# The first AdaLN shift as TensorE products, row by row with the first norm, in a float32 transformer kernel

## The chip, the cores and the metric

One core of a Trainium2 chip runs the whole program in one launch. The metric is the device time in microseconds of one execution, the median of several. The core has five engines with queues of their own: TensorE (PE; matmuls, with a weight load PEld for each), VectorE (DVE), ScalarE (ACT), GpSimd (POOL) and SyncE (SP, which here issues all the transfers from HBM). They meet only at semaphores.

## The reference

Three transformer blocks on x of 256 positions by 1024 features, in float32. The two first blocks are modulated by a vector c. What matters here:

```python
cond = jax.nn.silu(c)                                   # (1, 1024)
for l in range(2):
    m = (cond @ w_mod[l] + b_mod[l]).reshape(bsz, 3, 3, D_MODEL)
    x = x + 0.5 * m[:, 0, 2][:, None] * swiglu(adaln_in(x, norm_g[l, 0], m, 0), w1, w3, w2)
    ...

def adaln_in(x, g, m, i):
    return rmsnorm(x, g) * (1 + m[:, i, 1][:, None]) + m[:, i, 0][:, None]

def swiglu(h, w1, w3, w2):
    return (silu(h @ w1) * (h @ w3)) @ w2
```

Each layer needs 9 x 1024 modulation values: for each of its three sublayers a shift (index 0), a scale (1) and a gate (2), each value a dot product of 1024 terms with the silu of c. The first feed-forward layer (FFN 0) can't begin before its 1024 shifts and 1024 scales are known.

## The kernel before, in words

Features lie on the 128 partitions in 8 chunks, positions along the free axis: X is 128 x (8 x 256). A float32 product is made of three fp32r products: ScalarE rounds a block of weights into its high part WH (the split, L1287), VectorE makes the low part WL (L1860), activations have XH and XL likewise, and TensorE adds XH WH, XL WH and XH WL. WH and WL hold four units of 128 x 1024 each.

All weights come as one stream of items of up to 128 x 3072 (1.5 MB), in the order in which they are used, and SyncE issues them one after another; a wait in front of one holds up all behind it. FFN item c holds w1 and w3 of hidden chunk c and w2 of chunk c-1, and goes to one of three slots of `ring` (L611). FFN item 0 has only w1 and w3, 1 MB. Between them come modulation items (L600): three rows each, a row being the 128 x 1024 block whose 128 sums give one column of `modv`. They go to the slots scr (two of them), PR, att and kf_mix, which later hold other data, and item 5 borrows the third slot of `ring`. Items 0 to 5 make up the head: the first 8 rows of the stream are the shifts of sublayer 0, the next 8 the scales, then 2 rows of gates.

On VectorE `mod_row` (L1910 to 1923) handles a row by one multiply-and-reduce with the silu of c (`cond`, broadcast to all partitions), line L1916. For the head it does 16 of them one after another, then `scale_rates` (L1925) makes the gains adav, `norm_scale` (L1891) scales the 8 chunks of X by gain and reciprocal root into SQ, ScalarE adds the shift and rounds to XH (L1338, the high), VectorE makes XL (L1907, the low). The root itself is ScalarE's: squares (L1311), summed over features by TensorE with a matrix of ones (L674), then logarithm and exponential (L1325, L1328).

TensorE in the head: the sum of the squares, 8 `keep_warm` matmuls on constants (L668) in three groups behind waits, and then `head_up` (L719): 16 products XH WH chunk by chunk (L726), 16 XH WL (L731), 16 XL WH (L736). From chunk 1 of the FFN on, `up` (L691, L692, L695) and `down` (L785, L787, L792) alternate. ScalarE rounds FFN item c+1 before the silu of chunk c, and VectorE takes three more modulation rows for each chunk between its lows, gate rows of the head first. The wait in front of FFN item 2 (L609) is for the last scale row:

```python
i = PLACE[name]
if i == RING - 1:
    sp.wait_ge(*at("scale_row_read"))
```

Of the kernel before, what the change touches and what calls it, by code (L numbers as in the profile page):

```python
# [26 lines left out]
HEAD_MODS = 6  # L27
PADL, PADR = 3, 3
# [11 lines left out]
def columns(spec):  # L40
# [8 lines left out]
    ("b_mod", 144), ("norm_g", 48), ("a_qg", 1), ("a_kg", 1), ("c_qg", 1), ("c_kg", 1),  # L49
# [144 lines left out]
def build(nc, stream, param_d, const_d, bias_d, filter_d, x_d, mem_d, pos_d, c_d, out_d, known):  # L194
# [83 lines left out]
    def landed(name):  # L278
# [3 lines left out]
        if name[0] == "mod":  # L282
            k = MOD_SLOT[name[1]]
            return sig.sem(f"mod_landed{k}"), 16 * sum(MOD_SLOT[i] == k for i in range(name[1] + 1))
# [39 lines left out]
    def low_of(u):  # L324
        return f"low_{low_engine(u)}", u

# [252 lines left out]
    with nc.Block() as block:  # L579
# [3 lines left out]
        def _(sp):  # L583
            sp.dma_start(cond[:, :], c_d.partition_broadcast(P)).then_inc(*mark("c_in", n=16))
            sp.dma_start(par[:, :], param_d).then_inc(*mark("par_in", n=16))
            for name, n in ITEMS:
                if name[0] == "mod":
# [11 lines left out]
                    n = D if i == HEAD_MODS - 1 else n  # L599
# [15 lines left out]
                if name == ("ffn", 0, 0):  # L615
                    i = HEAD_MODS - 1
                    sp.wait_ge(*at("mod_read", 0))
                    sp.dma_start(mod_slots[0][:, D:ITEM], stream[ITEM_AT["mod", i], :, D:ITEM]).then_inc(*mark("gate_rows_in", n=16))
                if name == ("mod", 1):
                    sp.dma_start(con[:, 0:2 * P], const_d[:, 0:2 * P]).then_inc(*mark("ones_in", n=16))  # L620
                if name == ("mod", 3):
                    sp.dma_start(X, x_d).then_inc(*mark("x_in", n=16))
                if name == ("ffn", 0, 2):
                    sp.wait_ge(*at("mod_read", 4))
# [24 lines left out]
        def _(pe):  # L649
# [27 lines left out]
            def ffn(f):  # L677
# [41 lines left out]
                def head_up(b, units):  # L719

                    for k in range(KD):
                        pe.wait_ge(*at("norm_high", key, k))
                        for a, u in units:
                            if k == 0:
                                pe.wait_ge(*at("high", u))
                            pe.matmul(b[:, a * S:(a + 1) * S], part(WH, u, k), XH[:, k, :], start=(a == 0 and k == 0), stop=False,  # L726
                                      skip_group_check=True)
                    for a, u in units:
                        pe.wait_ge(*at(*low_of(u)))
# [1999 lines left out]
```

## Time and profile before

| what | value |
|---|---|
| median of 3 runs | 1420.14 us (1418.20 to 1420.48) |
| the profiled execution | 1419.84 us |
| its span, first to last instruction | 1418.0 us |
| TensorE busy | 1353.5 us, 95% |
| VectorE, ScalarE, GpSimd busy | 1089.7, 692.5, 53.8 us |
| moved by DMA | 305.79 MB, mean 216 GB/s |
| granted TensorE clock, mean | 0.992 of full |

Times of the trace are counted from the start of the span; the execution lasts 1.84 us longer than its span. Busy times overlap between engines, so they don't add up to the span. An engine that shows idle time is late only if the next thing on the chain of waits is its own.

### The profile page before, as it was taken

How to read it: one execution, taken by the hardware profiler on the slowest of the kernel's cores; microseconds unless marked ns; L12 is line 12 of the kernel's file. 1: busy time of each engine (PE TensorE's matmuls, PEld its weight loads, DVE VectorE, ACT ScalarE, POOL GpSimd, SP SyncE). 2: the span in 40 equal slices, each digit the busy share in tenths (PEclk: the TensorE clock that was granted, in tenths of full speed). 3: DMA queues.
4: the chain of work that ended last, by engine and by line, in shares of the span. 5: the costliest groups of instructions: out<-in, count | busy, mean ns of one | idle time of the engine just before them, and what ended most of it. 6: DMA issues, size and time to landing. Idle time of an engine off the chain costs nothing.

```text
span 1418.0 us, 26072 instructions
## 1 busy us (share of the span) xinstructions
PE 1353.5 (95%) x10734; PEld 1290.7 (91%) x10734; DVE 1089.7 (77%) x1835; ACT 692.5 (49%) x1120; POOL 53.8 (4%) x57
## 2 busy tenths in 40 slices
PE   2999999999999999999999999999999989999998
PEld 2999999889999999999998799999997868899998
DVE  6888999987787889878778866565678767677776
ACT  3443435555443363334465553344487756544453
POOL 0000000001000000001000020000010030100000
PEclk9999999999999999999999999999999999999999
DMA  9997758256768576574753145655422324245551
GB/s 392 409 388 288 309 187 337 104 192 277 304 267 317 217 289 267 223 326 172 283 200 134 60 179 216 240 194 212 176 93 105 119 78 175 90 178 182 186 196 62
DMA packets 32182, 305.79 MB, mean 216 GB/s; under 512 B 3480, under 2 KB 5784, under 8 KB 7360
## 3 DMA queue, kind: packets, MB, share of 16 engines
q1 hardware_dynamic: 32064, 304.13, 55.7%
q8 instruction: 85, 1.39, 0.4%
q14 instruction: 33, 0.27, 0.1%
HBM read 303.05 MB, written 1.06 MB: 214 GB/s over the span
## 4 chain that ended last, share of the span: by engine, by line
PE 83%; DVE 8%; DMA 3%; ACT 3%; issue 2%; POOL 1%; SPq 0%; POOLq 0%; DVEq 0%; ACTq 0%
PE bank L695 14%; PE bank L691 13%; PE bank L692 13%; PE bank L868 13%; PE bank L787 7%; PE bank L785 7%; PE bank L792 6%; DVE WL L1860 2%; DMA kf_mix<-in_stream 2%; PE bank L674 2%; DMA ring<-in_stream 1%; PE bank L709 1%; PE bank L941 1%; PE bank L715 1%; PE bank L952 1%
## 5 line engine op out<-in xcount | busy, mean ns | idle before, releaser
L1860 DVE TENSOR_TENSOR WL<-ring,WH 128x1024 fp32r<-128x1024 f32 x414 | 496.7, 1223 | 58.4 <-ACT WH L1287 56.2
L1287 ACT ACTIVATE WH<-ring 128x1024 fp32r<-128x1024 f32 x414 | 424.5, 1054 | 137.1 <-PE bank L868 51.9
L691 PE MATMUL bank<-XH,WH 128*128 128x256 f32 x1648 | 401.6, 282 | 0.6 <-ACT WH L1287 0.6
L692 PE MATMUL bank<-XL,WH 128*128 128x256 f32 x1648 | 400.0, 281 | 0.0
L691 PEld LDWEIGHTS bank<-XH,WH 128*128 128x128 f32 x1648 | 310.1, 188 | 6.5 <-issue 6.0
L692 PEld LDWEIGHTS bank<-XL,WH 128*128 128x128 f32 x1648 | 310.1, 188 | 0.5 <-issue 0.5
L695 PE MATMUL bank<-XH,WL 128*128 128x256 f32 x1648 | 229.9, 282 | 2.1 <-DVE WL L1860 2.1
L695 PEld LDWEIGHTS bank<-XH,WL 128*128 128x128 f32 x1648 | 210.2, 189 | 2.3 <-DVE WL L1860 2.3
L785 PE MATMUL bank<-GH,WH 128*128 128x256 f32 x840 | 203.6, 280 | 0.0
L787 PE MATMUL bank<-GL,WH 128*128 128x256 f32 x840 | 203.4, 280 | 0.0
L1372 ACT ACTIVATE SG<-bank 128x256 f32<-128x256 f32 x84 | 32.3, 384 | 340.7 <-PE bank L695 336.3
L787 PEld LDWEIGHTS bank<-GL,WH 128*128 128x128 f32 x840 | 158.5, 189 | 0.0
L785 PEld LDWEIGHTS bank<-GH,WH 128*128 128x128 f32 x840 | 158.4, 189 | 0.0
L1987 DVE TENSOR_TENSOR tmp<-SG,bank 128x256 f32<-128x256 f32 x88 | 37.0, 421 | 135.8 <-ACT SG L1372 134.8
L792 PE MATMUL bank<-GH,WL 128*128 128x256 f32 x808 | 111.4, 279 | 0.0
L792 PEld LDWEIGHTS bank<-GH,WL 128*128 128x128 f32 x808 | 102.2, 188 | 0.0
L868 PE MATMUL bank<-XH,WH 128*128 128x256 f32 x512 | 84.4, 290 | 4.2 <-ACT XH L1336 1.4
L868 PEld LDWEIGHTS bank<-XH,WH 128*128 128x128 f32 x512 | 70.6, 188 | 11.8 <-issue 7.8
L868 PE MATMUL bank<-XH,WL 128*128 128x256 f32 x512 | 80.1, 282 | 0.0
L1973 DVE SCALAR_TENSOR_TENSOR scr<-bank,par,scr 128x255 f32<-128x255 f32 x88 | 38.5, 478 | 46.8 <-ACT scr L1362 46.1
L1809 POOL TENSOR_TENSOR SQ<-SQ 128x256 f32<-128x256 f32 x35 | 36.9, 1055 | 935.1 <-ACT SQ L1311 934.0
L868 PE MATMUL bank<-XL,WH 128*128 128x256 f32 x512 | 71.5, 282 | 0.0
(321 smaller groups left out, 1598.5 us busy)
## 6 DMA issues: line engine op xcount, KB each, us to landing
ring<-in_stream SPq DMA_DIRECT2D x128, 1536.0 KB, 6.6
scr<-in_stream SPq DMA_DIRECT2D x15, 1536.0 KB, 9.9
PR<-in_stream SPq DMA_DIRECT2D x15, 1536.0 KB, 9.6
att<-in_stream SPq DMA_DIRECT2D x15, 1536.0 KB, 9.8
ring<-in_stream SPq DMA_DIRECT2D x12, 1024.0 KB, 4.9
ring<-in_stream SPq DMA_DIRECT2D x10, 512.0 KB, 3.6
kf_mix<-in_stream SPq DMA_DIRECT2D x2, 1536.0 KB, 16.9
con<-in_consts SPq DMA_DIRECT2D x1, 1680.0 KB, 20.0
```

The costliest lines, as they stand in the source:

```text
L691: pe.matmul(o, part(WH, u, k), XH[:, k, :], start=(k == 0), stop=False)
L692: pe.matmul(o, part(WH, u, k), XL[:, k, :], start=False, stop=False)
L695: last = pe.matmul(o, part(WL, u, k), XH[:, k, :], start=False, stop=(k == KD - 1))
L785: pe.matmul(out(m), part(WH, u, m), GH[:, c % 2, :], start=(c == 0 and m % 2 == 0), stop=False, skip_group_check=True)
L787: pe.matmul(out(m), part(WH, u, m), GL[:, c % 2, :], start=False, stop=False, skip_group_check=True)
L792: last = pe.matmul(out(m), part(WL, u, m), GH[:, c % 2, :], start=False, stop=False, skip_group_check=True)
L868: last = pe.matmul(bank[b][:, 0:S], part(w, u, blk + k), x[:, k, :], start=(opens and k == (ks or [0])[0]), stop=(p == parts[-1] and k == ...
L1287: act.activation(part_all(WH, u), raw(u), ACT.Copy).then_inc(*mark("high", u))
L1809: ins = pool.tensor_tensor(SQ[:, 0, :], SQ[:, 0, :], SQ[:, c, :], ALU.add)
L1860: dve.tensor_tensor(part_all(WL, u), raw(u), part_all(WH, u).bitcast(F32), ALU.subtract)\
L1973: ins = dve.scalar_tensor_tensor(o, src, prm("fconv_w", 2 * NFF * k + col), o, ALU.mult, ALU.add)
L1987: dve.tensor_tensor(G32[h], SG[h, c % 2, :], second, ALU.mult).then_inc(*mark("g32", f, c))
```

## The change

The 1024 shifts of sublayer 0 are no longer reduced on VectorE. Their weights lie in the stream as 8 blocks of 8 x (128 x 128), with the contracted features on partitions. POOL fills `wide`, the last 1024 columns of kf_mix, with the silu of c, each feature's value repeated over 128 columns (eight operations). TensorE multiplies: eight matmuls of 128 columns in plain float32 for each block of 128 shifts, which gives the block's shifts in each of the 128 columns; ScalarE adds b_mod to one column of them. The scales stay reductions on VectorE.

The stream's head alternates scale row and shift row. Each row is a transfer of its own (512 KB) into one of 16 places, in flight up to six at a time: row j waits until row j-6 is used. x, the ones and FFN item 0 are issued ahead of them. The first norm goes chunk by chunk on all engines as the rows come, with the products of FFN chunk 0 in between; the keep-warm matmuls of the head are removed.

The waits in SyncE's queue ahead of the items behind the head are for the single rows that used their places, and for the last row on the same semaphore.

SyncE, from the start of the program, before (slots scr, PR, att, kf_mix and ring; `mod_read` is a modulation item reduced, `low_dve` a low made):

```order
L584 DMA cond<-in_c 128x1024
L585 DMA par<-in_params 128x570
L600 DMA scr<-in_stream 128x3072 x2
L620 DMA con<-in_consts 128x256
L600 DMA PR<-in_stream 128x3072
L600 DMA att<-in_stream 128x3072
L622 DMA X<-in_x 128x2048
L600 DMA kf_mix<-in_stream 128x3072
L600 DMA ring<-in_stream 128x1024
L611 DMA ring<-in_stream 128x2048
L618 DMA scr<-in_stream 128x2048 [waits mod_read]
L600 DMA PR<-in_stream 128x3072 [waits mod_read]
```

and now, from the rows on (rows 0 to 15, of which six are left out, the gate rows, modulation item 6, FFN item 1, modulation item 7, FFN item 2):

```order
L610 DMA scr<-in_stream 128x1024 x6
L610 DMA PR<-in_stream 128x1024 [waits scale_in]
L610 DMA PR<-in_stream 128x1024 [waits shift_sum]
...
L610 DMA ring<-in_stream 128x1024 [waits shift_sum]
L613 DMA scr<-in_stream 128x2048 [waits shift_sum,scale_in]
L634 DMA PR<-in_stream 128x3072 [waits scale_in,shift_sum]
L645 DMA ring<-in_stream 128x3072
L634 DMA att<-in_stream 128x3072 [waits shift_sum,scale_in]
L645 DMA ring<-in_stream 128x3072 [waits shift_sum]
```

Six rows start freely, ten wait each for a row six places earlier, and modulation item 6 (PR, L634), with FFN item 1 behind it, waits for rows as well: for the reduction of row 14 (`scale_in`) among them.

TensorE's head, now (kf_mix is `wide`, scr and PR hold shift rows):

```order
L701 MATMUL bank<-SQ,con 128x256 [waits squared] x7
L754 MATMUL bank<-kf_mix,scr 128x128 [waits c_wide,mod_landed1]
L754 MATMUL bank<-kf_mix,scr 128x128 x7
L754 MATMUL bank<-kf_mix,scr 128x128 [waits mod_landed3]
L754 MATMUL bank<-kf_mix,scr 128x128 x7
L764 MATMUL bank<-XH,WH 128x256 [waits high,norm_high]
...
L754 MATMUL bank<-kf_mix,scr 128x128 [waits mod_landed5,shift_in]
L754 MATMUL bank<-kf_mix,scr 128x128 x7
L764 MATMUL bank<-XH,WH 128x256 [waits norm_high]
L764 MATMUL bank<-XH,WL 128x256
```

The products of a chunk (and the low products of the one before) now stand between two shift products, which share one in-order queue with them; 64 shift matmuls came in and 8 keep-warm ones went.

The diff, cut to its core, in the order of the file (SyncE, TensorE, ScalarE, POOL, VectorE):

```diff
+    def front_row(n):
+        a = (n % MOD_ROWS) * D
+        return mod_slots[n // MOD_ROWS][:, a:a + D]
+    wide = kf_mix[:, 3 * D:4 * D]
...
+            sp.dma_start(con[:, 0:2 * P], const_d[:, 0:2 * P]).then_inc(*mark("ones_in", n=16))
+            sp.dma_start(X, x_d).then_inc(*mark("x_in", n=16))
+            first = ("ffn", 0, 0)
+            sp.dma_start(slot(first), stream[ITEM_AT[first], :, 0:COLS[first]]).then_inc(sig.sem("slot_landed0"), 16)
+            for j in range(2 * KD):
+                if j >= FRONT:
+                    sp.wait_ge(*at("shift_sum" if j % 2 else "scale_in", (j - FRONT) // 2))
+                a = (j % MOD_ROWS) * D
+                sp.dma_start(front_row(j), stream[ITEM_AT["mod", j // MOD_ROWS], :, a:a + D]).then_inc(*mark(f"mod_landed{j % FRONT}", j, n=16))
...
-                        sp.wait_ge(*at("mod_read", HEAD_MODS - 1 if p == 0 else p))
+                        for w in front_read(p) if p < HEAD_MODS else [("mod_read", p)]:
+                            sp.wait_ge(*at(*w))
+                        if p < HEAD_MODS:
+                            j = max(j for j in range(2 * KD) if j % FRONT == k)
+                            sp.wait_ge(*at("shift_sum" if j % 2 else "scale_in", j // 2))
...
                     if i == RING - 1:
-                        sp.wait_ge(*at("scale_row_read"))
+                        sp.wait_ge(*at("shift_sum", KD - 1))
...
+                    def shift(k):
+                        take(k % 2, "shift_in", k)
+                        pe.wait_ge(*at(f"mod_landed{(2 * k + 1) % FRONT}", 2 * k + 1))
+                        if k == 0:
+                            pe.wait_ge(*at("c_wide"))
+                        for d in range(KD):
+                            last = pe.matmul(bank[k % 2][:, 0:P], front_row(2 * k + 1)[:, d * P:(d + 1) * P], wide[:, d * P:(d + 1) * P],
+                                             start=(d == 0), stop=(d == KD - 1))
+                        last.then_inc(*mark("shift_sum", k))
...
+                    for k in range(KD):
+                        shift(k)
+                        if k > 0:
+                            products(k - 1)
+                        if k > 1:
+                            low_products(k - 2)
+                    products(KD - 1)
+                    low_products(KD - 2)
+                    low_products(KD - 1)
...
             norm(("sub", 0, 0))
-            keep_warm(3)
-            pe.wait_ge(*at("stat_root", ("sub", 0, 0)))
-            keep_warm(3)
-            pe.wait_ge(*at("ada_in", 0, 0))
-            keep_warm(2)
...
+                for k in range(KD):
+                    act.wait_ge(*at("scale_in", k))
+                    g = prm("norm_g", k)
+                    act.activation(adav[:, 0, 0, k:k + 1], modv[:, KD + k:KD + k + 1], ACT.Identity, scale=g, bias=g)\
+                        .then_inc(*mark("rate_in", k))
+                    act.wait_ge(*at("shift_sum", k))
+                    act.activation(modv[:, k:k + 1], bank[k % 2][:, 0:1], ACT.Identity, bias=prm("b_mod", k))\
+                        .then_inc(*mark("shift_in", k))
+                    if k > 0:
...
+                        highs(k0, [k - 1])
...
+            for d in range(KD):
+                ins = pool.tensor_scalar(wide[:, d * P:(d + 1) * P], ones, prm("c_cols", d), None, ALU.mult)
...
+            def front_norm():
+                k0, (u0, u1) = ("sub", 0, 0), up_units(0, 0)
+                scale_row(0)
+                split_to(u0)
+                scale_row(1)
+                split_to(u1)
+                norm_root(k0)
+                for k in range(1, KD + 1):
+                    if 1 < k < KD:
+                        scale_row(k)
+                    dve.wait_ge(*at("rate_in", k - 1))
+                    norm_scale(k0, [k - 1])
+                    if k > 1:
+                        norm_lows(k0, [k - 2])
+                norm_lows(k0, [KD - 1])
```

## Rows read from the trace of the kernel before

**Rows 1.** The page, busy us by engine (share of the span, instructions).

```profile
PE 1353.5 (95%) x10734; PEld 1290.7 (91%) x10734; DVE 1089.7 (77%) x1835; ACT 692.5 (49%) x1120; POOL 53.8 (4%) x57
```

**Rows 2.** Stages: length, busy PE, PEld, DVE, ACT, POOL, clock, DMA share, GB/s.

```profile
10.00:20.00 10.00, 0.00 (x0) 0.00 (x0) 9.77 (x17) 0.00 (x0) 0.00 (x0) 1.00 1.01 426
...
28.00:31.00 3.00, 2.66 (x16) 2.26 (x16) 3.00 (x7) 0.89 (x2) 0.00 (x0) 1.00 0.99 421
...
40.00:50.00 10.00, 9.63 (x80) 9.33 (x79) 5.85 (x10) 4.64 (x6) 0.00 (x0) 1.00 1.02 378
```

**Rows 3.** Timeline of SyncE's queue: start us, us, queue, line, issue.

```profile
21.62 0.43 SPq L611 DMA_DIRECT2D ring<-in_stream  x1
...
32.23 0.33 SPq L611 DMA_DIRECT2D ring<-in_stream  x1
```

**Rows 4.** Timeline of ScalarE, 23 to 51 us; in brackets idle before, and releaser.

```profile
23.64 2.56 ACT L1311 ACTIVATE SQ<-X 128x256 f32<-128x256 f32 x8 [16.15 <-DMA X<-in_x]
...
29.81 0.47 ACT L1325 ACTIVATE tmp<-bank,par 128x256 f32<-128x256 f32 x1 [2.31 <-PE bank L674]
...
31.02 2.00 ACT L1287 ACTIVATE WH<-ring 128x1024 fp32r<-128x1024 f32 x2 [0.29 <-DMA ring<-in_stream]
...
41.03 2.01 ACT L1287 ACTIVATE WH<-ring 128x1024 fp32r<-128x1024 f32 x2 [4.68 <-DMA ring<-in_stream]
...
49.99 1.06 ACT L1287 ACTIVATE WH<-ring 128x1024 fp32r<-128x1024 f32 x1 [4.30 <-DMA ring<-in_stream]
```

**Rows 5.** Chain that ended last, 0 to 75 us: start us, us, what.

```profile
5.07 22.20 DMA kf_mix<-in_stream
...
29.79 1.20 DVE kf_mix L1916
...
32.23 17.74 DMA ring<-in_stream
```

**Rows 6.** Timeline of TensorE, 29 to 60 us.

```profile
29.61 0.83 PE L668 MATMUL bank<-con 128*128 128x128 f32 x6
...
39.54 2.23 PE L736 MATMUL bank<-XL,WH 128*128 128x256 f32 x16
...
49.83 1.10 PE L792 MATMUL bank<-GH,WL 128*128 128x256 f32 x8
...
51.19 0.36 PE L691 MATMUL bank<-XH,WH 128*128 128x256 f32 x1 [0.26 <-ACT WH L1287]
...
58.23 1.69 PE L695 MATMUL bank<-XH,WL 128*128 128x256 f32 x8 [2.06 <-DVE WL L1860]
```

**Rows 7.** Timeline of VectorE: first reduction, scaled chunks, lows of the third FFN chunk.

```profile
9.96 1.28 DVE L1916 CUSTOM_DVE_ANT_0 scr<-scr,cond,par 128x1024 f32<-128x1024 f32 x1 [9.96 <-DMA scr<-in_stream]
...
32.52 3.26 DVE L1895 SCALAR_TENSOR_TENSOR SQ<-X,adav,tmp 128x256 f32<-128x256 f32 x8
...
65.11 2.35 DVE L1860 TENSOR_TENSOR WL<-ring,WH 128x1024 fp32r<-128x1024 f32 x2
```

**Rows 8.** Single lines: count, ns min/median/max, first and last start.

```profile
L1392 ACT ACTIVATE rates<-rates x1: 212/212/212, 168.0 to 168.0; 128x8 f32<-128x8 f32 x1
...
L1809 POOL TENSOR_TENSOR SQ<-SQ x35: 721/746/1473, 226.0 to 1220.0; 128x256 f32<-128x256 f32 x35
```

**Rows 9.** The page, DMA issues: count, KB each, median us to landing.

```profile
ring<-in_stream SPq DMA_DIRECT2D x128, 1536.0 KB, 6.6
...
ring<-in_stream SPq DMA_DIRECT2D x10, 512.0 KB, 3.6
```

**Rows 10.** Stages again, for the granted clock (third number from the end).

```profile
35.00:38.00 3.00, 3.00 (x15) 3.00 (x16) 3.00 (x5) 1.35 (x4) 0.00 (x0) 0.50 1.00 421
...
60.00:62.00 2.00, 2.00 (x11) 2.00 (x11) 2.00 (x4) 2.00 (x3) 0.00 (x0) 0.50 1.04 442
...
230.00:235.00 5.00, 3.95 (x33) 3.79 (x33) 4.34 (x11) 4.42 (x11) 0.00 (x0) 1.00 1.00 391
1095.00:1100.00 5.00, 3.72 (x10) 2.91 (x11) 3.64 (x7) 4.94 (x6) 0.00 (x0) 0.64 0.38 160
```

More of the change, by code:

```diff
@@ L27 @@
 HEAD_MODS = 6
+FRONT = 6
 PADL, PADR = 3, 3
@@ L283, in landed @@
             k = MOD_SLOT[name[1]]
-            return sig.sem(f"mod_landed{k}"), 16 * sum(MOD_SLOT[i] == k for i in range(name[1] + 1))
+            front = sum(j % FRONT == k for j in range(2 * KD))
+            return sig.sem(f"mod_landed{k}"), 16 * (front + sum(MOD_SLOT[i] == k for i in range(HEAD_MODS, name[1] + 1)))
         i = PLACE[name]
@@ L719, in head_up, with products, low_products @@
                 def head_up(b, units):
-                    for k in range(KD):
+                    def shift(k):
[7 more added lines that the diff above has]
+                        last.then_inc(*mark("shift_sum", k))
+                    def products(k):
                         pe.wait_ge(*at("norm_high", key, k))
                         for a, u in units:
[L724 to L729, printed above, removed]
-                        for k in range(KD):
-                            pe.matmul(b[:, a * S:(a + 1) * S], part(WL, u, k), XH[:, k, :], start=False, stop=False,
-                                      skip_group_check=True)
-                    for k in range(KD):
+                            for which, w in ((WH, ("high", u)), (WL, low_of(u))):
+                                if k == 0:
+                                    pe.wait_ge(*at(*w))
+                                pe.matmul(b[:, a * S:(a + 1) * S], part(which, u, k), XH[:, k, :],
+                                          start=(which is WH and a == 0 and k == 0), stop=False, skip_group_check=True)
+                    def low_products(k):
                         pe.wait_ge(*at(*normed(key, k)))
@@ L1328, in root, with highs @@
                 act.activation(norm_rstd(k), norm_rstd(k), ACT.Exp, scale=-0.5).then_inc(*mark("stat_root", k))
-            def highs(k):
+            def highs(k, which=None):
                 N = NORMS[k]
-                for c in range(N["n"]):
+                for c in which or range(N["n"]):
                     act.wait_ge(*at("scaled", k, c))
@@ L1619, in _ @@
             act.activation(cond[:, :], cond[:, :], ACT.Silu).then_inc(*mark("cond"))
+            act.activation(prm("c_cols", 0, 8), prm("c_cols", 0, 8), ACT.Silu).then_inc(*mark("c_cols"))
+            def front_norm():
+                k0, (u0, u1) = ("sub", 0, 0), up_units(0, 0)
+                load_rates()
+                squares(k0, lambda c: [("x_in",)])
+                split_to(u0)
+                root(k0)
+                split_to(u1)
[8 more added lines that the diff above has]
+                    if k > 0:
+                        if k == 1:
+                            act.wait_ge(*at("shift_in", 0))
+                        act.wait_ge(*at("shift_in", k - 1))
+                        highs(k0, [k - 1])
+                act.wait_ge(*at("shift_in", KD - 1))
+                highs(k0, [KD - 1])
+                split_to(u1)
             for l in range(2):
                 if l == 0:
-                    norm(("sub", 0, 0), lambda c: [("x_in",)], ahead=up_units(0, 0)[1])
+                    front_norm()
                 else:
@@ L1896, in norm_scale, with norm_lows @@
                                              ALU.mult, ALU.mult).then_inc(*mark(*scaled(k, c)))
-            def norm_lows(k):
+            def norm_lows(k, which=None):
                 N = NORMS[k]
-                for c in range(N["n"]):
+                for c in which or range(N["n"]):
                     dve.wait_ge(*at("norm_high", k, c))
@@ L2622, in lay_out @@
     put_p("b_mod", feature_cols(f["b_mod"]))
+    put_p("c_cols", feature_cols(f["c"]))
     put_p("norm_g", feature_cols(f["norm_g"]))
@@ L2659, in lay_out @@
             blocks["mod", MOD_ITEMS * l + k] = m[k]
+    m = f["w_mod"][0]
+    rows = []
+    for k in range(KD):
+        rows.append(m[:, D + k * P:D + (k + 1) * P].T)
+        rows.append(m[:, k * P:(k + 1) * P].reshape(KD, P, P).transpose(1, 0, 2).reshape(P, D))
+    rows += [m[:, 2 * D + k * P:2 * D + (k + 1) * P].T for k in range(2)]
+    for k in range(HEAD_MODS):
+        blocks["mod", k] = np.stack(rows[MOD_ROWS * k:MOD_ROWS * (k + 1)], 1)
     def ffn(n, w1, w3, w2):
```

48 lines of the change are left out of this document (27 added, 21 removed).

## The prediction

> **What bounds the kernel now.** The page comes first: the span is 1418.0 us and TensorE is busy 95% of it [rows 1], so over the whole run only less TensorE work, or less TensorE waiting, shortens it. The edit removes hardly any work, so the question is what TensorE waits for near the start. The stage table answers: from 10 us on, and still at 40 to 50, the DMA engines are busy all the time, at 426 and 378 GB/s [rows 2]. That is a full pipe: what lands by when is set by the bytes ahead of it. The queue of SyncE shows FFN items 1 and 2 issued at 21.62 and 32.23 us [rows 3], and ScalarE waits for items 0, 1 and 2 to land: 31.02, 41.03 and 49.99 us [rows 4]. The chain of waits agrees: the kf_mix item, reductions behind it, then a DMA from 32.23 that takes 17.74 [rows 5]; its last waits lie at 51 and 58 us, and from there on TensorE has no gap worth naming. So the span is "landing of FFN item 2, plus a fixed rest", and FFN item 1 has no slack ahead of it either: the head's last products start at 39.54 and take 2.23 (to 41.77), item 1's first product needs the split that starts at 41.03 and takes 1.06 [rows 4, 6].
>
> **What the change can't give.** Ahead of FFN item 1 stand the same bytes before and after: c, parameters, ones, x, FFN item 0, sixteen rows of 512 KB, gate rows, modulation item 6. The eight VectorE reductions that go (1.20 us apart [rows 5]) were done while the pipe filled. Finishing the head sooner than 41.77 therefore gives nothing: item 1 can't land before 41.03. What the change can do is leave the pipe empty, because rows 6 to 15, and above all the PR item (modulation item 6) with FFN item 1 behind it, are now issued only after waits on single rows.
>
> **When the waits open.** Arrival is no limit: row 15 has the same bytes ahead of it as FFN item 0 had, so it would land at 31.0 and row 14 at 29.8 (512 KB at 426 GB/s is 1.23 us). x now has 2.0 MB up to its end against 2.4 MB for the first scr item, which landed at 9.96 [rows 7], so x lands at about 9.0. Squares to summed norm took 29.81-23.64 = 6.17 us [rows 4], so the sum is ready at 15.15. TensorE then does shift products 0 and 1. Each is 8 f32 matmuls of 128 columns, two records each; six such records took 0.83 [rows 6], hence 0.11 apart with a tail of 0.17. So 32 records take 3.5 us, and shift sum 1 is there at 18.8. (Row 3 is there at about 16.4; ScalarE's split of w3 ends at 17.2, VectorE's low of it at 18.4, its first scaled chunk at 18.8.)
> From there a loop closes: shift product k, ScalarE's bias copy of one column, ScalarE's high of chunk k-1, then TensorE's four products of chunk k-1 and two low ones, which stand ahead of shift product k+1. One turn is 16x0.11+0.17 = 1.93, the copy 0.25 (0.21 from SBUF [rows 8], taken a little higher from PSUM), the high 0.44 and six products 0.71 (eight take 1.10, of which the last 0.28 [rows 6]: 0.118 each), and hand-overs 0.15: **3.5 us per row pair** against 2.46 us of DMA. Shift sum 2 comes at 22.0, 4 at 29.0, 5 at 32.5. VectorE needs 1.20+0.41+0.41 = 2.0 per turn (0.41 for a scaled chunk [rows 7], and as much for a low) but waits for the same highs: row 14's reduction follows the low of chunk 4, so it ends at 32.5+0.25+0.44+0.45+1.28 = 34.9.
> That frees the PR item: its wait names the reduction of row 14. The pipe is dry by then: row 15 is issued at shift sum 4 (29.0), the gate rows behind it, 1.5 MB, done by about 34. The PR item and FFN item 1 go out together at 35.0. From an empty pipe 512 and 1536 KB take 3.6 and 6.6 us to land [rows 9], which is 2.4 and 2.9 us plus the bytes; 3 MB need 2.4+7.4 = 9.8, so item 1 lands at 44.8 instead of 41.03: **+3.7 us**. FFN item 2 is free at shift sum 7 (39.5), while the pipe is still full, and is late by the same 3.7; so is the rest.
>
> **What TensorE's clock gives back.** TensorE finishes the head at about 41.3 and idles until 45.8. After its 2 us idle at 56 to 58 the granted clock was 0.50 from about 58.6 to 62.2, the lower level of 1.2 GHz, and likewise around 35 to 38 after a stretch of short pieces [rows 10]; either costs half of 3.4 us, 1.7. I take it that item 1's products run at the lower level for as long. That is covered: two waits stand behind them, 0.26 us at 51.19 and 2.06 us at 58.23, where VectorE's low of w3 is last [rows 6]. With 1.7 of these 2.3 us used up, only 0.6 us of idling is left at that place, and gaps of 0.3 to 0.6 at 41.8 and 51 brought no fall of the clock. So the fall at 58.6 goes: **-1.7 us**. VectorE keeps up: the low of the next w3 (65.11 and the 1.2 of the first of the pair [rows 7], plus 3.7: 70.0) is ready when TensorE wants it, at about 70.2.
>
> **The small parts.** The eight broadcasts of POOL start when the ones and the silu of c are there (7.7) and must end by 15.15. At 0.75 us, the median of POOL's two-input operations of twice the columns [rows 8], they end at 13.7: hidden. At the 1.47 us of the slowest of these they end at 19.5 and cost up to 4 us: kept for the range. Nothing here excludes either. ScalarE's 16 one-column activations are in the loop above; the extra silu and the eight removed keep-warm matmuls lie beside waits. Rows of 4 KB a partition instead of 12 KB: nothing, since while the 512 KB row and the 1 MB item drained before 31 us the pipe moved 421 GB/s [rows 2]. The Trainium skill ("DMA: Bandwidth & Descriptors", on the latency of a transfer) gives each DMA about 2 us of fixed cost beside its bytes; paid one after another by sixteen rows, the sum by that page would hold an estimated 32 us more. In this trace such costs overlap while several transfers are queued: the DMA share is full [rows 2].
>
> **The sum.** 1419.84 + 3.7 - 1.7 = 1421.8. The profiled execution is 0.3 below the median of 1420.14; I put the median to come at **1422.0**. A measurement of this kernel can tell about 0.2%, 2.8 us, from no change: no change lies between 1417.3 and 1423.0. The DMA term's ends: 0 if the loop keeps up with arrival (reduction of row 14 at 31.05, plus 9.8, is 40.9), and +16 if each turn ran at the lower clock (1.93 and 0.71 doubled: 5.9 us a turn; shift sum 5 near 46).
>
> **The rivals.**
> 1. *The pipe stays full* (0.11). If a turn takes 2.5 us, item 1 lands at 41.0 to 42.5, and with the second fall of the clock gone or not the time is 1418.5 to 1420.5. For it: VectorE's 2.0 us a turn. Against: the products alone are 2.6 us of a turn.
> 2. *The clock falls in the head: slower* (0.22). TensorE works some 2.7 of 3.5 us. It held the full clock at 3.95 of 5 us busy, and lost it at 3.72 of 5 [rows 10]. It decides as soon as one fall lies between 19 and 32 us: each adds up to 1.7 us to the loop and so to the landing, two or three give 1424 to 1428. The late POOL broadcast ends in the same place. The Trainium skill ("TensorE: Matmul & The Clock Gate", Part 1) says that the lower clock is the default and that only activity lifts it. By that rule the head's pauses speak for this rival. Rows 10 show a case of either kind.
> 3. *The fall at 58 us stays* (0.15): item 1's products start at full clock, or the wait at 58 keeps its 2 us. Then nothing is given back: 1423.5.
> 4. *Faster by over 0.2%* (0.06): landings come out earlier than bytes allow at 426 GB/s, or both falls go and VectorE's chain after 50 us shortens too: 1416.
> The forecast case (item 1 late by 2.5 to 4.9 us, the fall gone: 1420.6 to 1423.2) has 0.46.
>
> **How the numbers follow.** Range: 1418.8 to 1427.0. It leaves out about half of rival 4 and of rival 1's lower end, and the tail of rival 2. Within 0.2%: nearly all of the forecast case and rival 1, 0.55. Slower: rivals 2 and 3 and a rest, 0.38. Faster: 0.07.
>
> **What would show it.** In the profile after: x lands near 9 and the norm's sum ends near 15; shift products come 3.5 us apart; SyncE issues PR at about 35 with a dip of the DMA share just then; ScalarE's wait for FFN item 1 ends near 44.8 and for item 2 near 53.7; a lower clock at 45 to 49 and none at 62. I am wrong if the DMA share has no dip between 22 and 37 us, if turns are nearer 2.5 or 5 us, or if w1 of item 2 is not later than 49.99.

## Result, and the profile after

| what | before | after |
|---|---|---|
| median of 4 runs each, one chip | 1420.06 us | **1427.35 us** (1426.14 to 1429.87) |
| ratio | | 1.0057 [1.0045, 1.0069] |
| the profiled execution, its span | 1419.84, 1418.0 us | 1428.07, 1426.1 us |
| TensorE busy | 1353.5 us | 1369.9 us |
| granted clock, mean | 0.992 | 0.992 |

The change makes the kernel slower by 7.3 us. The forecast was 1422.0, with a range up to 1427.0. A slower kernel had been given a chance of 0.38; the size lies outside the range.

The page of the changed kernel, span and busy times (they answer to [rows 1]):

```profile
span 1426.1 us, 26338 instructions
PE 1369.9 (96%) x10846; PEld 1307.5 (92%) x10846; DVE 1079.8 (76%) x1818; ACT 696.6 (49%) x1137; POOL 58.4 (4%) x65
```

The head first. Timeline of SyncE's queue in the changed kernel (start us, us, queue, line, issue), to set beside [rows 3]:

```profile
29.54 0.33 SPq L610 DMA_DIRECT2D ring<-in_stream  x1
29.98 0.36 SPq L613 DMA_DIRECT2D scr<-in_stream  x1
35.52 0.33 SPq L634 DMA_DIRECT2D PR<-in_stream  x1
35.90 0.43 SPq L645 DMA_DIRECT2D ring<-in_stream  x1
```

Row 15 and the gate rows go out at 29.5 and 30.0, then nothing until 35.52, where the PR item and FFN item 1 follow. Timeline of ScalarE after, against [rows 4]:

```profile
15.69 0.47 ACT L1364 ACTIVATE tmp<-bank,par 128x256 f32<-128x256 f32 x1 [2.79 <-PE bank L701]
...
26.05 0.26 ACT L1674 ACTIVATE modv<-bank,par 128x1 f32<-128x1 f32 x1 [2.59 <-PE bank L754]
...
29.55 0.26 ACT L1674 ACTIVATE modv<-bank,par 128x1 f32<-128x1 f32 x1 [2.57 <-PE bank L754]
...
45.62 2.00 ACT L1326 ACTIVATE WH<-ring 128x1024 fp32r<-128x1024 f32 x2 [4.49 <-DMA ring<-in_stream]
...
54.59 1.06 ACT L1326 ACTIVATE WH<-ring 128x1024 fp32r<-128x1024 f32 x1 [4.32 <-DMA ring<-in_stream]
...
72.67 0.38 ACT L1411 ACTIVATE SG<-bank 128x256 f32<-128x256 f32 x1 [0.22 <-PE bank L722]
```

The copies that add the bias to two neighbouring shifts (26.05, 29.55) lie 3.50 us apart: one turn of the loop. FFN items 1 and 2 land at 45.62 and 54.59, 4.6 us later than before (41.03, 49.99). The stages after (columns as in [rows 2]):

```profile
14.00:20.00 6.00, 5.25 (x41) 4.88 (x39) 5.24 (x8) 3.19 (x8) 0.00 (x0) 1.00 1.03 411
20.00:26.00 6.00, 5.25 (x42) 4.88 (x42) 4.90 (x11) 1.32 (x4) 0.00 (x0) 1.00 1.02 392
...
34.00:36.00 2.00, 2.00 (x19) 2.00 (x19) 1.83 (x4) 0.00 (x0) 0.00 (x0) 1.00 0.51 213
36.00:38.00 2.00, 1.25 (x11) 1.06 (x11) 0.74 (x2) 0.93 (x3) 0.00 (x0) 1.00 0.78 188
...
46.00:48.00 2.00, 1.27 (x6) 1.27 (x7) 1.29 (x2) 1.98 (x3) 0.00 (x0) 0.50 1.05 449
...
60.00:62.00 2.00, 2.00 (x20) 2.00 (x19) 1.93 (x6) 0.29 (x1) 0.00 (x0) 1.00 0.95 390
```

The pipe of transfers runs dry at 34 to 38 us (213 and 188 GB/s). TensorE's granted clock is 0.50 at 46 to 48 and full at 60 to 62, where [rows 10] had 0.50.

So far this is the forecast. Its price shows where the silu of each FFN chunk starts, since that follows the chunk's last product. The silu of chunk 0 is 4.59 us later than before, that of chunk 3 only 3.13 (72.67 against 69.54). But from there the difference grows without a new wait in the head: 4.1 us at 215 us, 4.8 at 529, 5.8 at 1016, 8.05 at the last chunk, near 1409. Of these 4.9 us, 4.5 come in FFN 0, 1, 3 and 4, 0.06 us with each chunk. The rest isn't even: between 1118 and 1234 us, ahead of FFN 4, another 1.4 come, where the granted clock was at 0.50 for 10.2 us instead of 6.8, and the remaining stretches take 1.0 back. Two rows of ScalarE's timeline before, two neighbouring chunks:

```profile
103.62 0.39 ACT L1372 ACTIVATE SG<-bank 128x256 f32<-128x256 f32 x1 [4.58 <-PE bank L695]
112.14 0.38 ACT L1372 ACTIVATE SG<-bank 128x256 f32<-128x256 f32 x1 [4.57 <-PE bank L695]
```

and the same chunks after:

```profile
106.98 0.39 ACT L1411 ACTIVATE SG<-bank 128x256 f32<-128x256 f32 x1 [4.57 <-PE bank L722]
115.56 0.39 ACT L1411 ACTIVATE SG<-bank 128x256 f32<-128x256 f32 x1 [4.57 <-PE bank L722]
```

A chunk took 8.52 us and takes 8.58, with the same instructions. TensorE's timeline shows which of them grew. The first row is the first of the 16 `down` products with WH, the second the 8 with WL behind them. Before:

```profile
121.60 0.28 PE L785 MATMUL bank<-GH,WH 128*128 128x256 f32 x1
...
123.48 1.10 PE L792 MATMUL bank<-GH,WL 128*128 128x256 f32 x8
```

After:

```profile
125.09 0.28 PE L829 MATMUL bank<-GH,WH 128*128 128x256 f32 x1
...
127.01 1.12 PE L836 MATMUL bank<-GH,WL 128*128 128x256 f32 x8
```

The sixteen take 1.88 us before and 1.92 after, at a granted clock of 1.00 in both. By the mean distance from one product's start to the next one's, between 100 and 220 us: the products of `up` have 118.3 to 118.9 ns in both kernels, those of `down` 117.9, 117.8 and 117.8 before (GH WH, GL WH, GH WL), and 121.3, 118.8 and 120.2 after. With the 840, 840 and 808 of them that is an estimated 2.8 + 0.8 + 1.9 = 5.6 us (with the unrounded means). It is more than the 4.5 us that the chunks show, since in FFN 2 (529 to 716 us) the difference hardly grows.

No wait of the head reaches so far. What can is in a line that my prediction passed over, and that the cut diff doesn't show: the vector c that POOL reads as `c_cols` is 8 new columns of the parameter tile `par` (570 to 578 columns).

```diff
-    ("b_mod", 144), ("norm_g", 48), ("a_qg", 1), ("a_kg", 1), ("c_qg", 1), ("c_kg", 1),
+    ("b_mod", 144), ("c_cols", 8), ("norm_g", 48), ("a_qg", 1), ("a_kg", 1), ("c_qg", 1), ("c_kg", 1),
```

The tiles are laid out one behind another, so every tile behind `par` begins 32 bytes further on: XH and XL, GH and GL among them, but not WH and WL.

### The profile page after: what moved, and what is told of

The parts are those of the page before. It is cut to its first block, busy times and chain, and to the rows that moved or that the text cites. A ratio compares the mean times of both kernels' runs of the same rounds, so it can differ in the third digit from the quotient of the medians.

```text
span 1426.1 us, 26338 instructions
## 1 busy us (share of the span) xinstructions
PE 1369.9 (96%) x10846; PEld 1307.5 (92%) x10846; DVE 1079.8 (76%) x1818; ACT 696.6 (49%) x1137; POOL 58.4 (4%) x65
## 4 chain that ended last, share of the span: by engine, by line
PE 87%; DVE 6%; ACT 3%; issue 2%; DMA 1%; POOL 1%; POOLq 0%; DVEq 0%; SPq 0%; ACTq 0%
PE bank L912 14%; PE bank L722 13%; PE bank L718 13%; PE bank L719 13%; PE bank L829 7%; PE bank L831 7%; PE bank L836 7%; PE bank L701 2%; DVE WL L1930 1%; PE bank L736 1%; PE bank L754 1%; DMA ring<-in_stream 1%; PE bank L985 1%; PE bank L742 1%; PE bank L996 1%
## 5 line engine op out<-in xcount | busy, mean ns | idle before, releaser
L719 PE MATMUL bank<-XL,WH 128*128 128x256 f32 x1648 | 401.2, 282 | 0.0
L722 PEld LDWEIGHTS bank<-XH,WL 128*128 128x128 f32 x1648 | 210.6, 189 | 0.7 <-DVE WL L1930 0.7
L831 PE MATMUL bank<-GL,WH 128*128 128x256 f32 x840 | 206.3, 282 | 0.0
L912 PEld LDWEIGHTS bank<-XH,WL 128*128 128x128 f32 x512 | 71.2, 191 | 0.3 <-issue 0.2
```

The source lines that it names most:

```text
L719: pe.matmul(o, part(WH, u, k), XL[:, k, :], start=False, stop=False)
L722: last = pe.matmul(o, part(WL, u, k), XH[:, k, :], start=False, stop=(k == KD - 1))
L831: pe.matmul(out(m), part(WH, u, m), GL[:, c % 2, :], start=False, stop=False, skip_group_check=True)
L912: last = pe.matmul(bank[b][:, 0:S], part(w, u, blk + k), x[:, k, :], start=(opens and k == (ks or [0])[0]), stop=(p == parts[-1] and k == ...
```

## The experiments

Three theories at the start. **A**: the head costs some 3 us, and the rest is where the operand tiles lie. **B**: the rest comes with the longer program, wherever the tiles lie. **C**: it is something else that the new head leaves behind. Beside them, that the growth is chance of one profile. Each ratio below is to the kernel before on the same chip, with its 95% interval.

### The tiles moved, the head left alone

```diff
-    ("eps", 1), ("inv", 1), ("halfpi", 1), ("tiny", 1)])
+    ("eps", 1), ("inv", 1), ("halfpi", 1), ("tiny", 1), ("spare", 8)])
```

> The kernel before with 8 unused columns at the end of its parameter tile, and nothing else: every tile that is allocated behind it lies 32 bytes later, as in the changed kernel. In the changed kernel an FFN chunk of 72 products takes 8.58 us instead of 8.52, over some 84 chunks, about 5 us. Theory A (the place of the operands in memory): this kernel takes 1425 us, 5.0 more than before, and its chunks take 8.58. Theory B (the longer TensorE program) and theory C (something that the new head leaves behind): it takes 1420.1, chunks at 8.52.

Measured: 1423.63 us (11 runs), ratio 1.0026 [1.0018, 1.0035]. Chunks take 8.58 us, `down` products 121.4 and 120.2 ns; the difference to before is 0.5 us at chunk 3 and 5.4 at the last. Eight unused columns, and no change of the head, give the growth from chunk to chunk. By the runs they cost 3.7 us [2.6, 5.0]; the profiled execution is the slowest of the 11.

### The changed kernel with its tiles back in place

In the changed kernel, ("spare", 56) at the same place: 64 new columns in all, so every tile has the place it had before, give or take a whole 256 bytes.

> The changed kernel with 56 unused columns at the end of its parameter tile, so that all tiles behind it lie 256 bytes later than in the kernel before instead of 32. Theory A: chunks at 8.52 again, 1422.3 us, 5.0 less than the changed kernel; what is left against before, about +2 to +3, is the head. Theories B and C: no change, 1427.3.

Measured: 1423.92 us (9 runs), ratio 1.0028 [1.0018, 1.0038]. Chunks take 8.52 us; the difference is 2.7 us at chunk 3 and 3.0 at the last. The groups of TensorE in the changed kernel (line, products | busy us, mean ns of one):

```profile
L829 PE MATMUL bank<-GH,WH 128*128 128x256 f32 x840 | 206.2, 284 | 0.0
...
L836 PE MATMUL bank<-GH,WL 128*128 128x256 f32 x808 | 113.5, 282 | 0.0
```

and of this kernel:

```profile
L829 PE MATMUL bank<-GH,WH 128*128 128x256 f32 x840 | 202.5, 279 | 0.0
...
L836 PE MATMUL bank<-GH,WL 128*128 128x256 f32 x808 | 111.4, 279 | 0.0
```

So C is out: the new head with the tiles back in place has no growth. The parts add up within their intervals: the head alone 0.28%, the place alone 0.26%, together 0.54% beside 0.57 measured. By the runs the head costs 4.0 us [2.6, 5.4], by this one profile 3.0.

### A longer program without the tiles moved

```diff
             pe.wait_ge(*at("ones_in"))
+            keep_warm(56)
             norm(("sub", 0, 0))
```

> The kernel before with 56 more matmuls on constants ahead of the sum of the squares, while TensorE has nothing to do: as many as the changed head has more. Theory B (TensorE's program is longer, so later instructions lie elsewhere in it): chunks of 8.58 us and 1425 us. Theories A and C: 1420.1, since the 56 matmuls end before x lands.

Measured: 1418.84 us (11 runs), ratio 0.9998 [0.9990, 1.0007]; chunks take 8.52 us. TensorE has the 10846 instructions of the changed kernel here, so B is out, and chance was out with the first experiment. In this profile the clock is 1.00 at 35 to 38 and at 60 to 62 us, where [rows 10] had 0.50; the silu of chunk 0 came 1.2 us later all the same, that of chunk 3 0.9 sooner. That the 56 matmuls held the clock isn't shown: the kernel with 8 unused columns, which lacks them, has 1.00 at 35 to 38 us as well (and 0.50 at 60 to 62).

### Which tile it is

The same 8 columns in the kernel before, but behind XH and XL and ahead of GH and GL:

```diff
     adav = sb("adav", 2 * 3 * 16)[:, :].rearrange("p (i k c) -> p i k c", k=2, c=8)
+    spare = sb("spare", 8)
     SG, GH, GL = chunks("SG", 2), chunks("GH", 2, F32R), chunks("GL", 2, F32R)
```

> The kernel before with 8 unused columns allocated just ahead of SG, GH and GL: only these tiles and those behind them lie 32 bytes later; XH, XL, SQ, kf_mix, PR and scr stay. In the changed kernel the 24 products on GH and GL took about 120 ns each from start to start instead of 117, those on XH and XL about 118 in both. Theory A1 (the place of GH and GL): chunks of 8.58 us and 1423.7, as with the 8 columns at the parameters. Theory A2 (the place of XH and XL, or of others ahead): 8.52 and 1419.2.

Measured: 1423.85 us (6 runs), ratio 1.0036 [1.0024, 1.0049]. `up` products as before (118.4 to 118.8 ns), GH WH at 121.0 and GH WL at 120.2. A chunk takes 8.57 us, and 8.58 where XH and XL move too. So it is the place of GH and GL that costs, and the 32 bytes of XH and XL next to nothing. GH and GL moved together, and the profile doesn't part them: between 1240 and 1400 us GH WH takes 116.7 ns and GL WH 122.3. SG and the tiles behind moved as well, but no `down` product reads them. (This profile, at 1428.11 us, is far above its median: between 1121 and 1241 us its clock was at 0.50 for 17 us, and the stretch took 3.8 us longer than before.)

### FFN item 1 ahead of the PR item

In the changed kernel SyncE issues FFN item 1 and then modulation item 6, everything else in place.

```diff
-            for name, n in ITEMS:
+            issues = list(ITEMS)
+            at6 = issues.index((("mod", HEAD_MODS), ITEM))
+            issues[at6:at6 + 2] = issues[at6:at6 + 2][::-1]
+            for name, n in issues:
```

> The changed kernel with one swap in SyncE's queue: FFN item 1 is issued ahead of modulation item 6, whose wait for row 14 it does not share. Theory of the dry pipe: item 1 is issued at 30 instead of 35.9 us and lands by 38, the DMA share stays full from 34 to 38, chunk 1 starts at about 42.8 instead of 46.7, right behind the head, and FFN item 2 lands 2 us sooner than 54.59; whether TensorE then loses its clock at the wait for item 2 decides between 1425.3 us (not) and 1427 us (it does). Rival, the pipe is not what holds item 1 (TensorE's head does): no change, 1427.3.

Measured: 1424.64 us (5 runs), ratio 1.0035 [1.0021, 1.0049]; 1427.35 for the changed kernel. Item 1 goes out at 29.56 and the silu of chunk 0 comes at 43.67 instead of 48.94. Item 2 lands only at 53.53 (54.59 after). The stages of this kernel:

```profile
50.00:52.00 2.00, 0.36 (x4) 0.16 (x2) 0.00 (x0) 0.00 (x0) 0.00 (x0) 1.00 1.03 232
52.00:54.00 2.00, 0.00 (x0) 0.00 (x0) 0.00 (x0) 0.47 (x1) 0.00 (x0) 0.94 1.05 399
54.00:56.00 2.00, 1.27 (x6) 1.30 (x7) 1.39 (x2) 2.00 (x4) 0.00 (x0) 0.50 0.99 420
```

TensorE stands still for 4 us ahead of item 2 instead of item 1, and the fall of the clock moves with the gap. In the profile 5.3 us gained at chunk 0 are 0.8 at chunk 3: item 2's landing binds, and the bytes ahead of it are the same. By the medians 2.7 us are gained, though the intervals of the two ratios overlap; of the 2.0 that this profile gains in all, 1.4 are the stretch near 1200 us, where its clock was low for 6.8 us again.

### The loop opened

To the kernel with its tiles back in place: four banks for the shift sums instead of two, and products one row pair further behind.

```diff
-                        take(k % 2, "shift_in", k)
+                        take(k % 4, "shift_in", k)
...
                         shift(k)
-                        if k > 0:
-                            products(k - 1)
                         if k > 1:
-                            low_products(k - 2)
+                            products(k - 2)
+                        if k > 2:
+                            low_products(k - 3)
```

> The changed kernel with the 56 unused columns and with TensorE's head in another order: four banks for the shift sums instead of two, and the products of chunk k-2 (not k-1) behind shift product k, so that TensorE no longer waits in each turn for ScalarE's high of the chunk before. Theory of the closed loop: a turn falls from 3.5 to about 2.5 us, the bound of arrival; row 14's reduction ends near 32 instead of 35.4, FFN item 1 lands near 42.5 instead of 45.6 and item 2 near 51.5 instead of 54.6; 1421, 3 less than with the columns alone (1423.9). Rival (arrival of the smaller rows or VectorE holds the turn at 3 us and more): 1422.5 to 1423.9.

Measured: 1420.54 us (11 runs), ratio 1.0007 [0.9998, 1.0016], 3.4 us under the same kernel with the closed loop (1423.92, another chip; by the ratios 3.0). ScalarE's timeline:

```profile
27.58 0.26 ACT L1676 ACTIVATE modv<-bank,par 128x1 f32<-128x1 f32 x1 [2.05 <-PE bank L754]
...
30.14 0.26 ACT L1676 ACTIVATE modv<-bank,par 128x1 f32<-128x1 f32 x1 [1.61 <-PE bank L754]
...
32.64 0.26 ACT L1676 ACTIVATE modv<-bank,par 128x1 f32<-128x1 f32 x1 [1.57 <-PE bank L754]
...
43.36 2.00 ACT L1328 ACTIVATE WH<-ring 128x1024 fp32r<-128x1024 f32 x2 [7.16 <-DMA ring<-in_stream]
...
52.01 1.06 ACT L1328 ACTIVATE WH<-ring 128x1024 fp32r<-128x1024 f32 x1 [4.00 <-DMA ring<-in_stream]
```

One turn is 2.5 us now, the pace of the rows, and the PR item goes out at 33.04 instead of 35.52. The silu of chunk 3 is 0.5 us behind the kernel before instead of 2.7. The closed loop was most of what the head cost.

### Both FFN items ahead of both modulation items

The same in the queue, with items 1 and 2 ahead of modulation items 6 and 7: once on the kernel just shown, once on the kernel before.

```diff
+            m6, f1, m7, f2 = issues[at6:at6 + 4]
+            issues[at6:at6 + 4] = [f1, f2, m6, m7]
```

> The kernel of the run before with FFN items 1 and 2 both issued ahead of modulation items 6 and 7, which VectorE needs only some 15 us later. If bytes ahead of item 2 are what holds the start, item 2 lands near 44 to 46 us, chunk 2 follows chunk 1 without a wait, and the silu of chunk 3 comes at about 66 instead of 69.5 as in the kernel before: 1416. Rival: VectorE, which has the gate rows and then three rows of item 6 to reduce between lows, or the later landing of items 6 and 7, becomes the bound: 1419 or more.

> The kernel before with the same swap of the queue, FFN items 1 and 2 ahead of modulation items 6 and 7, and no other edit. The head still ends at 41.8 us. If item 2's landing bounds, chunk 2 starts at about 50.6 without the waits at 51 and 58 us and the fall of the clock behind them: 1416 to 1417, about 3 less than before. If VectorE bounds there: 1419.

Measured on the changed kernel with the open loop: 1418.29 us (12 runs, 1416.06 to 1422.51), ratio 0.9996 [0.9986, 1.0006]. Item 1 lands at 38.91, but ScalarE waits 6.60 us for item 3 (to 56.39) and 8.18 us for item 4 (to 67.79), and the silu of chunk 3 is only 0.8 us ahead of before: 1418.29 lies between the 1416 of the theory and the rival's 1419. Measured on the kernel before: 1415.36 us (6 runs), ratio 0.9974 [0.9963, 0.9985]. Its ScalarE:

```profile
37.31 2.01 ACT L1291 ACTIVATE WH<-ring 128x1024 fp32r<-128x1024 f32 x2 [0.87 <-DMA ring<-in_stream]
```

and its stages:

```profile
35.00:38.00 3.00, 2.95 (x19) 2.34 (x18) 3.00 (x5) 2.13 (x5) 0.00 (x0) 1.00 1.03 429
50.00:52.00 2.00, 2.00 (x20) 2.00 (x19) 1.93 (x6) 0.00 (x0) 0.00 (x0) 1.00 1.01 430
58.00:60.00 2.00, 2.00 (x19) 2.00 (x18) 1.97 (x6) 0.39 (x1) 0.00 (x0) 1.00 0.99 414
```

The wait for FFN item 1, 4.68 us in [rows 4], is 0.87, and the fall of the clock at 60 us in [rows 10] is gone. (The fall at 35 is absent too, but it also is with 8 unused columns alone, so it says nothing on the queue.) At 215 us the kernel is 4.7 ahead. Two modulation items that VectorE first reads at 54.63 and 62.77 us in the kernel before stood in the queue ahead of FFN items 1 and 2, which TensorE waits for; this the change left as it was.

### Small rows

In the kernel before, items 0 to 4 of the head go as three transfers of 512 KB each.

```diff
-                    sp.dma_start(mod_slots[k][:, 0:n], stream[ITEM_AT[name], :, 0:n]).then_inc(sig.sem(f"mod_landed{k}"), 16)
+                    for a in range(0, n, D if i < HEAD_MODS - 1 else n):
+                        e = a + (D if i < HEAD_MODS - 1 else n)
+                        sp.dma_start(mod_slots[k][:, a:e], stream[ITEM_AT[name], :, a:e]).then_inc(sig.sem(f"mod_landed{k}"), 16)
```

> The kernel before with each of the head's five full modulation items moved as three transfers of 512 KB (4 KB a partition) instead of one of 1.5 MB, in the same order and with the same waits. In the changed kernel the pipe moved 303 to 420 GB/s between 16 and 28 us with a DMA share near 1. If the small rows themselves are slower, FFN item 1 lands 0.5 to 2 us later than 41.03 and the kernel takes 1420 to 1421; if not, that rate came from the waits and it takes 1419.2.

Measured: 1419.76 us (11 runs), ratio 1.0001 [0.9992, 1.0009]. At 10 to 20 us the pipe moves 415 GB/s instead of 426, and item 1 lands at 41.63, 0.6 later; in the measured time it can't be told from nothing.

### Other places

The place of GH and GL cost about 0.3%, so other places could give. All on the kernel before but the last. ("spare", 16) in `par`, 64 bytes:

> The kernel before with 16 unused columns at the end of its parameter tile: every tile behind lies 64 bytes later. If 32 bytes matter only because 64-byte steps of the place are equal, the chunks stay at 8.52 us and the time at 1419.2; if the place counts by 128 bytes, products on GH and GL or on XH and XL change from 117.8 or 118.5 ns, and a chunk by 0.02 to 0.06 us: 1421 to 1424, or 1417.

16 columns in `par` and 16 ahead of SG, first together with the queue order above, then alone:

> FFN items 1 and 2 ahead of modulation items 6 and 7, as in the best run so far (1415.4), with 16 unused columns at the parameters (XH and XL 64 bytes later) and 16 ahead of SG (GH and GL 128 bytes later). If XH and XL are read a little faster at a place like that of GH and GL in the kernel before (117.8 instead of 118.5 ns for 48 of 72 products), a chunk takes 8.49 and the kernel 1412.5; if not, 1415.4.

> The kernel before with 16 unused columns at the parameters and 16 ahead of SG, and SyncE's queue as it was. Theory: the 34.5 us between 1380.9 and 1415.4 come from the place of the tiles alone (chunks of 8.16 instead of 8.52 us), and the queue gives its 4 us beside: 1385. Rival: place and queue work together (the transfers meet the products), and without the queue's change it stays above 1395.

Another 32 bytes (24 and 16), and 16 ahead of SG alone:

> The same with 24 columns at the parameters: XH, XL, GH and GL each lie 32 bytes later than in the run beside it, so at a multiple of 32 bytes that is not one of 64. Theory: 32 bytes off is what costs, products of 120 ns and more as GH and GL had in the changed kernel, chunks of 8.5 us or more, 1420 or more. Rival: only the distance between tiles counts, then 8.16 and 1385.

> The kernel before with 16 columns ahead of SG only: XH and XL stay at a multiple of 128 bytes, GH and GL move to one. Theory (a tile 64 bytes off a multiple of 128 is the fast place): products on GH and GL go from 117.8 to 118.7 ns as in the run with 16 columns at the parameters, 1420 to 1422. Rival (XH and GH must lie alike within 256 bytes): chunks near 8.16 and 1385.

The changed kernel with 8 spare columns in `par` (16 with its own 8) and 16 ahead of SG:

> The changed kernel with its tiles at the same places as in the first run of this call (8 unused columns at the parameters beside its own 8, 16 ahead of SG). Theory: place and head add up, chunks of 8.16 and the head 3 to 4.5 us dearer than there: about 1389. Rival: nothing is left of the head's cost when TensorE is faster: 1385.

Places are given from the start of WH, as what is left over a multiple of 256 bytes. (In the built program WH itself begins at byte 37248, 128 past a multiple of 256, so each place counted from address 0 leaves 128 more.) Spacings are mean distances of starts between 100 and 220 us.

| kernel | XH, XL | GH, GL | `up`, ns | `down`, ns | us | ratio |
|---|---|---|---|---|---|---|
| before | 128 | 64 | 118.3-118.8 | 117.8-117.9 | 1418.92 to 1420.06, by chip | 1 |
| changed | 160 | 96 | 118.3-118.9 | 118.8-121.3 | 1427.35 | 1.0057 |
| before, 8 late | 128 | 96 | 118.4-118.8 | 117.3-121.0 | 1423.85 | 1.0036 |
| before, 16 in `par` | 192 | 128 | 115.5-116.1 | 118.6-119.0 | 1404.02 | 0.9892 [0.9878, 0.9907] |
| before, 16 and 16 | 192 | 192 | 113.3-113.4 | 113.3-113.4 | 1394.07 | 0.9823 [0.9788, 0.9857] |
| the same, items first | 192 | 192 | 113.3-113.4 | 113.3-113.4 | **1380.91** | 0.9739 [0.9715, 0.9764] |
| changed, 8 and 16 | 192 | 192 | 113.9-114.0 | 113.9-114.0 | 1385.51 | 0.9754 [0.9738, 0.9770] |
| before, 24 and 16 | 224 | 224 | 118.2-118.5 | 118.2-118.5 | 1420.67, one run | |
| before, 0 and 16 | 128 | 128 | 118.6-118.7 | 118.6-118.7 | 1423.91, one run | |

TensorE's timeline of the fastest kernel, to set beside the two fences above:

```profile
123.75 0.28 PE L790 MATMUL bank<-GH,WH 128*128 128x256 f32 x1
...
125.57 1.07 PE L797 MATMUL bank<-GH,WL 128*128 128x256 f32 x8
```

The sixteen products with WH take 1.82 us. Its page:

```profile
span 1377.5 us, 26072 instructions
PE 1309.8 (95%) x10734; PEld 1246.7 (91%) x10734; DVE 1087.7 (79%) x1835; ACT 691.6 (50%) x1120; POOL 54.3 (4%) x57
```

and two neighbouring chunks of it, 8.16 us apart:

```profile
132.11 0.38 ACT L1377 ACTIVATE SG<-bank 128x256 f32<-128x256 f32 x1 [4.32 <-PE bank L700]
140.27 0.38 ACT L1377 ACTIVATE SG<-bank 128x256 f32<-128x256 f32 x1 [4.32 <-PE bank L700]
```

It has TensorE busy for 43.7 us less than the kernel before with the same 10734 matmuls, and at 1380.91 us it beats both kernels.

Of the theories for these runs, most missed. The place was expected to move a chunk by 0.02 to 0.06 us, and it moved it by up to 0.36. "16 and 16" alone was put at 1385, or above 1395 if place and queue work together, and took 1394.07. The changed kernel at the same places was put at 1389, by the rival at 1385, and took 1385.51. So at this place the costs of head, queue and place no longer add up: the queue order is worth 0.26% at the old place and some 0.8% here (from two chips), and the changed kernel is quicker than the one before. The two places tried last have one run each. 224 and 224 took the time expected, but with products of 118 ns and not 120; 128 and 128 has the spacing expected and took 1423.91 for 1420 to 1422.

**What stays open.** The place decides how fast the products can be, but by which rule the table doesn't say. 192 and 192 is fast; yet GH at 64 gave 117.8 where XH was at 128, so a tile's own remainder modulo 128 is not enough: it may be modulo 256, or the two tiles together. Nor does the place decide alone. In the profile of "16 and 16" the chunks of FFN 0 and 4 take 8.16 us, but those of FFN 1 and 3 take 8.48, at a granted clock of 1.00 in all four. With the items first nearly all take 8.16. In the changed kernel at this place they go from 8.48 to 8.16 near 120 us, are at 8.48 again in FFN 1, and at 8.16 in FFN 3 and 4. The four runs of "16 and 16" spread from 1388 to 1401. Something tips a stretch from one spacing to the other, and no run here shows what; it may be why the costs don't add up, but that isn't shown either.

## Why the prediction was wrong, point by point

- **What bounds the kernel.** Right for the head: the landings of FFN items 1 and 2 set the time up to chunk 3, and moving item 1 alone brought 0.8 us at chunk 3, because item 2 then bound. "From there on TensorE has no gap worth naming" was right for the FFN chunks, and was the trap: the prediction took the span as the landing of FFN item 2 "plus a fixed rest", and where TensorE is busy 95% of the time, a rest is only fixed while the products keep their spacing.
- **When the waits open.** The turn came at 3.50 us as worked out. The norm's sum was ready at 15.69 (15.15 forecast), the PR item went out at 35.52 (35.0), and item 1 landed 10.1 us later (9.8). Together +4.6 instead of **+3.7**: the mechanism was right, the size short by 0.9. x had landed 0.3 late (9.31), and the squares began at 9.39. Rows of 512 KB moved 415 instead of 426 GB/s while they filled the pipe in the small-rows run, which I had costed at nothing; that run put 0.6 us on it in a profile. (A turn with both terms doubled is 6.1 us and not 5.9; it only set the far end of the DMA term.)
- **What the clock gives back.** The low clock at 46 came and that at 60 went, as forecast. The difference fell from 4.59 us at chunk 0 to 3.13 at chunk 3, so 1.5 came back instead of **1.7**. So the head's net cost is 3.1 us in the profile, 4.0 [2.6, 5.4] by runs, where the sum had 2.0. That is the smaller part of the miss, 1 to 2 us.
- **The small parts, and the fixed rest.** This is the step that failed. It costed POOL's eight broadcasts, and they are hidden as it said (8 in 4.65 us, from 8.18 on). It did not cost where they read from: eight columns added to `par`, which move every tile behind it by 32 bytes. The sum has no term for that, so it stood at nothing without a reason. The run with the eight columns alone puts 3.7 us [2.6, 5.0] on it, the larger part of the miss. With it the sum is 1421.8 + 1.1 for the head + 3.7 to 5.6 for the place, 1426.6 to 1428.5; the profiled execution took 1428.07.
- **The rivals.** Rival 1 (the pipe stays full) did not come; the open loop made its turn of 2.5 us, though item 1 landed at 43.4 there, not at 42.5 or sooner. Rival 2 (the clock falls in the head) did not come: the granted clock is 1.00 in all stages from 14 to 42 us. TensorE held the full clock with 5.25 and 4.51 of 6 us busy (20 to 26, 26 to 32 us), about the 2.7 of 3.5 that I had set, and lost it behind a stretch with 0.71 of 3 (42 to 45). The Trainium skill ("TensorE: Matmul & The Clock Gate", Part 1) has the lower clock as the default that activity lifts. The trace agrees behind the wait for FFN item 1 (0.50 at 46 to 48 us); no pause of the head shows a fall. Rival 3 (the fall at 58 stays) did not come, rival 4 neither. Rival 2 had been priced at 1424 to 1428, and the measured time lies there by luck: the slower side came from a cause that no rival had.

## What to carry to other kernels

Read an edit for what it does to the sizes of tiles, not only to instructions: a few columns in a parameter tile move everything allocated behind it, and where TensorE is the bound, 1 ns more on each of 10734 matmuls is an estimated 10.7 us of span. So compare two kernels at equal tile places (pad the change to a multiple of 256 bytes) before a difference is put down to the edit, and try the places on their own: here they were worth more than every reordering tried (1.8% for "16 and 16" alone, 0.26% for the queue order alone). A difference that grows by the same amount with each repetition has a cause in the steady state, whatever was edited at the start.

## What was not expected of the hardware

- The same fp32r products of 256 columns, each with a weight load of its own, start about 113.3, 116, 118 or 121 ns apart with the place of their operands, at the same granted clock of 1.00. With unused columns as the only edit, that is 1394.07 to 1423.91 us in the time. The Trainium skill ("TensorE: Matmul & The Clock Gate", Back-to-back issue gap) gives the isolated gap as the columns over 2.4 GHz plus 2.5 ns, an estimated 109.2 ns here, without a term for the operand's place. The trace comes no nearer than 113.3.
- A step of 32 bytes is enough for GH and GL, and costs (117.8 to about 120 ns); the same step of XH and XL, from 128 to 160, is not seen in their spacing (118.3 to 118.9 ns in either place).
- The low clock near 1200 us differs from profile to profile. The stretch between FFN 3 and 4 (1118 to 1234 us) takes 115.2 to 115.5 us in six profiles with 6.8 us of it at 0.50 (113.6 to 114.8 in three more, at other places), 116.3 to 116.9 in seven with 10.2 or 13.7 us, and 119.0 in the one with 17 us (8 late). So one profile can be 1 to 4 us longer by this alone, as much as the head or the place cost; whether an edit has a part in it isn't shown.
- In one profile, with every tile at one place, chunks of the same products took 8.16 us in two layers and 8.48 in two others ("16 and 16" alone), all at a granted clock of 1.00.
